# Four 128x512 reciprocals of a streaming mixer as logarithm and exponential on the activation engine

## The reference

```python
r = sigmoid(xc @ wa + ba);  i = sigmoid(xc @ wx + bx)        # xc: causal conv of the xl part, 512 wide
log_a = -8 * r * softplus(-lam);  a = exp(log_a)
mult = sqrt(-expm1(2 * log_a))
h[t] = a[t] * h[t-1] + mult[t] * i[t] * xc[t]                # linear recurrence over tokens
y_lru = h * gelu(gl)
hm = rmsnorm_per_head(mlstm_chunk(q, k, v, gates))           # 4 heads of 128
y_m = hm * mlstm_norm * sigmoid(o)
x = x + concat(y_lru, y_m) @ w_out
x = x + peer(rmsnorm(x))                                     # 8 heads, each the top 16 of 16384 experts
```

## Time and profile before

| | |
|---|---|
| time of three runs | median 3380.85 us (3374.79, 3380.85, 3388.64) |
| the profiled execution | 3388.64 us, span 3386.7 us |
| mean granted clock of TensorE in it | 0.976 |
| busy: PE, DVE, ACT, POOL | 2947.2, 2347.8, 662.4, 2015.6 us |

### The profile page before, as it was taken

One profiled execution on the slowest core, in us unless ns is written; L12 is line 12 of the kernel. 1 busy time (PEld: TensorE's weight loads), 2 busy tenths in 40 slices (PEclk: granted clock), 3 DMA queues, 4 the chain that ended last, 5 costly groups with the idle time before them and its releaser, 6 DMA issues.

```text
span 3386.7 us, 39112 instructions
## 1 busy us (share of the span) xinstructions
PE 2947.2 (87%) x10724; PEld 1546.2 (46%) x10724; DVE 2347.8 (69%) x5813; ACT 662.4 (20%) x2015; POOL 2015.6 (60%) x2132
## 2 busy tenths in 40 slices
PE   7687899888998899878998899888998899988777
PEld 2462464345543464445543455435543455444223
DVE  3474986678756886678756886578756786679553
ACT  2211221112211221112211122112211122111111
POOL 0133566656667566666667566665667566765775
PEclk9798999999999999999999999999999999999999
DMA  7455999999999999999999999999999999999998
GB/s 256 144 180 201 401 343 353 403 382 383 343 379 413 363 359 345 408 385 388 339 378 416 372 356 336 398 388 372 343 379 402 375 356 335 393 418 385 414 420 331
DMA packets 340167, 1213.76 MB, mean 358 GB/s; under 512 B 41072, under 2 KB 41200, under 8 KB 339904
## 3 DMA queue, kind: packets, MB, share of 16 engines
q0 software_dynamic: 304128, 1107.43, 85.0%
q1 hardware_dynamic: 35776, 103.32, 7.9%
HBM read 1205.73 MB, written 4.87 MB: 357 GB/s over the span
## 4 chain that ended last, share of the span: by engine, by line
PE 44%; DMA 19%; DVE 18%; issue 11%; POOL 4%; ACT 2%; POOLq 0%; DVEq 0%; SPq 0%; ACTq 0%
PE acc L428 27%; PE bank L428 17%; DMA ring<-peer_v,idx 16%; DVE ring L1272 5%; POOL ring L404 4%; DMA ring<-peer_u,idx 4%; ACT xn L755 1%; DVE kw L1056 1%; DVE xn L1167 1%; DVE xn L1170 1%; DVE topi L1058 1%; DVE eh L1067 1%; DVE kw L1066 1%; DVE tops L1057 1%; DVE bank L1180 1%
## 5 line engine op out<-in xcount | busy, mean ns | idle before, releaser
L428 PE MATMUL acc<-ring,diag 128*128 128x512 f32 (+1 forms) x4224 | 2039.6, 611 | 351.9 <-DMA ring<-peer_v,idx 225.8
L1272 DVE SCALAR_TENSOR_TENSOR ring<-ring,xcur 128x1024 f32<-128x1024 f32 x1056 | 1281.0, 1218 | 657.5 <-DMA ring<-peer_u,idx 648.6
L404 POOL DMA_INDIRECT ring<-peer_u,idx x1056 | 1016.0, 962 | 736.3 <-issue 284.8
L404 POOL DMA_INDIRECT ring<-peer_v,idx x1056 | 995.9, 943 | 614.5 <-issue 272.9
L428 PEld LDWEIGHTS acc<-ring,diag 128*128 128x128 f32 (+1 forms) x4224 | 731.8, 189 | 1312.1 <-issue 894.1
L755 ACT ACTIVATE diag<-ident,coef 128x128 f32<-128x128 f32 x1024 | 368.4, 395 | 618.3 <-PE acc L428 521.5
L428 PEld LDWEIGHTS bank<-xT,win 128*128 128x128 f32 (+1 forms) x2304 | 273.9, 184 | 76.6 <-issue 67.7
L428 PE MATMUL bank<-xT,win 128*128 128x128 f32 (+1 forms) x2304 | 284.9, 279 | 2.4 <-ACT xT L755 2.4
L755 ACT ACTIVATE G<-bank 128x128 f32<-128x128 f32 (+1 forms) x137 | 40.6, 296 | 667.0 <-PE bank L428 666.8
L428 PE MATMUL bank<-win,xT 128*128 128x512 f32 (+3 forms) x368 | 165.6, 581 | 1.9 <-ACT xT L755 1.9
L428 PEld LDWEIGHTS bank<-xT,qk 128*128 128x128 f32 x1024 | 130.1, 199 | 35.9 <-issue 35.9
(11 more groups left out here) (227 smaller groups left out, 1847.1 us busy)
## 6 DMA issues: line engine op xcount, KB each, us to landing
qk<-wq SPq DMA_DIRECT2D x64, 512.0 KB, 6.8
t<-wq SPq DMA_DIRECT2D x64, 512.0 KB, 6.6
ring<-peer_u,idx POOLq DMA_INDIRECT x1056, 6.3
ring<-peer_v,idx POOLq DMA_INDIRECT x1056, 6.3
win<-w_in SPq DMA_DIRECT2D x6, 2048.0 KB, 15.3
ring<-wq SPq DMA_DIRECT2D x16, 512.0 KB, 4.9
wout<-w_out SPq DMA_DIRECT2D x1, 4096.0 KB, 22.1
xn<-x_prompt SPq DMA_DIRECT2D x8, 512.0 KB, 9.2
```

The lines of the kernel that those rows point to most:

```text
L404: pool.indirect_dma_start(out=ring[:, slot, :], out_offset=None, in_=(peer_u, peer_v)[which], in_offset=bass.IndirectOffsetOnAxis(ap=idx[: ...
L428: return nc.tensor.matmul(out, lhsT, rhs, start=start, stop=stop)
L1272: stt(row, row, 1.0, xcur[:, :], ALU.mult, ALU.mult, accum_out=dots[:, column(b, e):column(b, e) + 1]).then_inc(s_dot, 1)
```

## The change

Each of the four reciprocals of 1 + e^-x over 128x512 (GELU, r, i, output gate) is taken from DVE. DVE still adds 1 (for three of them, with a clamp to 2^60 in the same instruction; for the GELU the 1 is the bias of the logarithm), and ACT computes exp(-ln(1 + e^-x)) in place. The chain behind r and i (t4, the series, the square root, the scan) and ACT's square root move two ticks later, ACT's exponential of the decay one tick later, the product with the GELU one tick later, and the add for the output gate five ticks earlier. The code is otherwise the same, two semaphores for each of i and the output gate are new (s_ri1, s_i, s_o1, s_so).

```diff
+            def logistic(t, bias):
+                link(a(t, t, ACT.Ln, bias=bias))
+                return a(t, t, ACT.Exp, scale=-1.0)
...
                 if full and tick == T_GELU + 2:
                     act.wait_ge(s_gl_arg, w + 1)
-                    a(t3[:, :, 0:n], t3[:, :, 0:n], ACT.Exp, scale=GELU_SCALE).then_inc(s_gl_exp, 1)
+                    link(a(t3[:, :, 0:n], t3[:, :, 0:n], ACT.Exp, scale=GELU_SCALE))
+                    logistic(t3[:, :, 0:n], 1.0).then_inc(s_gl_exp, 1)
...
                 if tick == T_LRU + 3:
-                    act.wait_ge(s_r, v + 1)
+                    act.wait_ge(s_ri1, v + 1)
+                    link(logistic(t1[:, :, 0:n], 0.0))
+                    act.sem_inc(s_r, 1)
+                    logistic(t2[:, :, 0:n], 0.0).then_inc(s_i, 1)
+                if tick == T_LRU + 4:
                     for f in range(FT):
                         last = a(t3[:, f, 0:n], t1[:, f, 0:n], ACT.Exp, scale=decay_c[:, f:f + 1])
                     last.then_inc(s_a, 1)
...
-                if tick == T_LRU + 10:
+                if tick == T_LRU + 12:
                     act.wait_ge(s_m2, v + 1)
...
+                if full and tick == T_CHUNK + 10:
+                    act.wait_ge(s_o1, w + 1)
+                    logistic(sigo[0:n, :, :], 0.0).then_inc(s_so, 1)
...
-                    ts(t3[:, :, 0:n], t3[:, :, 0:n], -50.0, None, ALU.max).then_inc(s_gl_arg, 1)
-                if full and tick == T_GELU + 3:
+                    ts(t3[:, :, 0:n], t3[:, :, 0:n], -26.0, None, ALU.max).then_inc(s_gl_arg, 1)
+                if full and tick == T_GELU + 4:
                     dve.wait_ge(s_gl_exp, w + 1)
-                    link(ts(t3[:, :, 0:n], t3[:, :, 0:n], 1.0, None, ALU.add))
-                    link(dve.reciprocal(t3[:, :, 0:n], t3[:, :, 0:n]))
                     link(tt(G[:, :, 0:n], G[:, :, 0:n], t3[:, :, 0:n], ALU.mult))
...
                 if tick == T_LRU + 2:
                     dve.wait_ge(s_ri_exp, v + 1)
-                    link(ts(t1[:, :, 0:n], t1[:, :, 0:n], 1.0, None, ALU.add))
-                    dve.reciprocal(t1[:, :, 0:n], t1[:, :, 0:n]).then_inc(s_r, 1)
-                if tick == T_LRU + 3:
-                    link(ts(t2[:, :, 0:n], t2[:, :, 0:n], 1.0, None, ALU.add))
-                    link(dve.reciprocal(t2[:, :, 0:n], t2[:, :, 0:n]))
-                if tick == T_LRU + 4:
+                    ts(t1[:, :, 0:n], t1[:, :, 0:n], 2.0 ** 60, 1.0, ALU.min, ALU.add)
+                    ts(t2[:, :, 0:n], t2[:, :, 0:n], 2.0 ** 60, 1.0, ALU.min, ALU.add).then_inc(s_ri1, 1)
+                if tick == T_LRU + 6:
                     dve.wait_ge(s_r, v + 1)
+                    dve.wait_ge(s_i, v + 1)
...
+                if full and tick == T_CHUNK + 8:
+                    dve.wait_ge(s_o, w + 1)
+                    ts(sigo[0:n, :, :], sigo[0:n, :, :], 2.0 ** 60, 1.0, ALU.min, ALU.add).then_inc(s_o1, 1)
...
                 if tick == T_CHUNK + 13:
-                    dve.wait_ge(s_o, w + 1)
-                    link(ts(sigo[0:n, :, :], sigo[0:n, :, :], 1.0, None, ALU.add))
-                    link(dve.reciprocal(sigo[0:n, :, :], sigo[0:n, :, :]))
+                    dve.wait_ge(s_so, w + 1)
```

More of the change, by code:

```diff
@@ L207, in program @@
         s_gl_ps, s_gl, s_gl_arg, s_gl_exp = sem("s_gl_ps"), sem("s_gl"), sem("s_gl_arg"), sem("s_gl_exp")
-        s_ri_ps, s_ri_exp, s_r, s_a, s_m2, s_mult, s_lru = (sem(f"s_{n}") for n in ("ri_ps", "ri_exp", "r", "a", "m2", "mult", "lru"))
+        s_ri_ps, s_ri_exp, s_ri1, s_i, s_r, s_a, s_m2, s_mult, s_lru = (sem(f"s_{n}") for n in ("ri_ps", "ri_exp", "ri1", "i", "r", "a", "m2", "mult", "lru"))
         s_q_ps, s_q, s_k_ps, s_k, s_v_ps, s_v = (sem(f"s_{n}") for n in ("q_ps", "q", "k_ps", "k", "v_ps", "v"))
@@ L212, in program @@
         s_kt_ps, s_kw, s_s_ps, s_p, s_num_ps, s_num, s_c_ps, s_c = (sem(f"s_{n}") for n in ("kt_ps", "kw", "s_ps", "p", "num_ps", "num", "c_ps", "c"))
-        s_o_ps, s_o, s_hsq, s_hrs, s_ym, s_ym_ps, s_ymT = (sem(f"s_{n}") for n in ("o_ps", "o", "hsq", "hrs", "ym", "ym_ps", "ymT"))
+        s_o_ps, s_o, s_o1, s_so, s_hsq, s_hrs, s_ym, s_ym_ps, s_ymT = (sem(f"s_{n}") for n in ("o_ps", "o", "o1", "so", "hsq", "hrs", "ym", "ym_ps", "ymT"))
         s_out_ps, s_h2, s_rstd2, s_xn2, s_x2_ps, s_x2 = (sem(f"s_{n}") for n in ("out_ps", "h2", "rstd2", "xn2", "x2_ps", "x2"))
@@ L1165, in mixer @@
                     dve.wait_ge(s_ri_exp, v + 1)
-                    link(ts(t1[:, :, 0:n], t1[:, :, 0:n], 1.0, None, ALU.add))
-                    dve.reciprocal(t1[:, :, 0:n], t1[:, :, 0:n]).then_inc(s_r, 1)
-                if tick == T_LRU + 3:
-                    link(ts(t2[:, :, 0:n], t2[:, :, 0:n], 1.0, None, ALU.add))
-                    link(dve.reciprocal(t2[:, :, 0:n], t2[:, :, 0:n]))
-                if tick == T_LRU + 4:
+                    ts(t1[:, :, 0:n], t1[:, :, 0:n], 2.0 ** 60, 1.0, ALU.min, ALU.add)
+                    ts(t2[:, :, 0:n], t2[:, :, 0:n], 2.0 ** 60, 1.0, ALU.min, ALU.add).then_inc(s_ri1, 1)
+                if tick == T_LRU + 6:
                     dve.wait_ge(s_r, v + 1)
+                    dve.wait_ge(s_i, v + 1)
                     link(tt(t4[:, :, 0:n], t1[:, :, 0:n], spread(decay_c[:, FT:2 * FT].unsqueeze(2), 2, n), ALU.mult))
                     tt(t2[:, :, 0:n], t2[:, :, 0:n], xc[:, :, 0:n], ALU.mult)
-                if tick == T_LRU + 5:
+                if tick == T_LRU + 7:
                     link(ts(by4(bA)[:, :, 0:n], t4[:, :, 0:n], 1.0 / 120, None, ALU.mult))
-                for at, c in ((5, -1.0 / 24), (6, 1.0 / 6), (6, -0.5), (7, 1.0)):
+                for at, c in ((7, -1.0 / 24), (8, 1.0 / 6), (8, -0.5), (9, 1.0)):
                     if tick == T_LRU + at:
                         link(stt(by4(bA)[:, :, 0:n], by4(bA)[:, :, 0:n], c, t4[:, :, 0:n], ALU.add, ALU.mult))
-                if tick == T_LRU + 7:
+                if tick == T_LRU + 9:
                     link(ts(t4[:, :, 0:n].bitcast(u32), t4[:, :, 0:n], 0.125, None, ALU.is_lt))
-                if tick == T_LRU + 8:
+                if tick == T_LRU + 10:
                     dve.wait_ge(s_a, v + 1)
@@ L1186, in mixer @@
                     link(ts(t1[:, :, 0:n], t1[:, :, 0:n], -1.0, 1.0, ALU.mult, ALU.add))
-                if tick == T_LRU + 9:
+                if tick == T_LRU + 11:
                     link(dve.copy_predicated(t1[:, :, 0:n], t4[:, :, 0:n].bitcast(u32), by4(bA)[:, :, 0:n]))
                     ts(t1[:, :, 0:n], t1[:, :, 0:n], 2.0 ** -60, None, ALU.max).then_inc(s_m2, 1)
-                if tick == T_LRU + 11:
+                if tick == T_LRU + 13:
                     dve.wait_ge(s_mult, v + 1)
@@ L1198, in mixer @@
                     link(last)
-                if tick == T_LRU + 12:
+                if tick == T_LRU + 14:
                     last = dve.tensor_copy(hst[:, :].unsqueeze(2), t4[:, :, n - 1:n])
```

## The result

The changed kernel takes 3391.33 us (median of 20 runs, 3380.88 to 3398.06), the kernel before 3380.26 us (20 runs): ratio 1.003, 95% interval 1.002 to 1.0041. It is a little slower, by 0.2 to 0.4%. The forecast was 3364 us with a range up to 3384; the result is outside it, on the side of the rival called slower, but not by that rival's mechanism. The profiled execution has a span of 3395.4 us, 8.7 us more than that of before.

A forecast was written before the change was run, and what follows sets the result against it. PE was taken to bound ticks 43 to 82 of a block, POOL's gather pace the last block. The terms +9.5 - 15.6 - 3 - 5.7 - 2 gave -16.8 us, 3364 us against the median 3380.85, range 3336 to 3384.

The forecast's parts named there:

- the rival called slower: New wait at tick 59 throttles TensorE's clock in every block: +2 us, up to +12.5 us (3393 us); chance 0.08.
- DVE loses: Four reciprocals and an add leave DVE per full mixer: 13.8 us in each of eight, 111 us busy time, mostly not gain.
- the likeliest range of the forecast: The main case, with the change -8 to -27 us faster; chance 0.62, half of it on either side of the 0.5% line.
- r and i, tick 59: ACT's added work delays a diagonal; PE's wait grows from 0.42 to about 1.8 us a block, +9.5 us over seven blocks.
- Tick 64: PE's wait there for DVE's late dots, about 2.2 us in each of seven blocks, goes: -15.6 us.
- Clock: Half-clock pieces after three tick-64 waits go, new tick-59 waits may bring one or two: -2 us (bounds -5 and +6).
- Output gate: POOL no longer waits for DVE at tick 87: -3 us of at most -5.4 over the loop, as PE bounds again soon after.
- Ahead of the loop: In the three mixers before the loop, reciprocals leave the serial chain, less a later diagonal: -5.7 us in sum.
- GELU and the chain behind r: ACT's longer GELU at tick 53 and the chain moved by two ticks are hidden in the loop: 0 us.
- DVE is the real bound: DVE's queue, not PE, sets the pace in ticks 43 to 82; half the possible gain is 37 us, 3338 us; chance 0.12.
- Given back: Tick-59 wait costs what tick 64 saves, POOL's gain is lost, only the start remains: 0 to -7 us, 3377 us; chance 0.18.
- The list of what would make the prediction wrong: Dot 63 not earlier, PE waiting at another diagonal (54, 68 or 85), or loop blocks shrinking by more than 3.7 us each.

The follow-up runs named there:

- e1: Changed kernel with 12 idle semaphore increments ahead of DVE's loop, restoring the loop top's old place 488; 3370.53 us, ratio 0.9961 to the kernel before.
- e8: Changed kernel with 60 idle semaphore increments ahead of DVE's loop, its top at place 536; 3368.3 us, ratio 0.995 to the kernel before.
- e11: Changed kernel with 6 idle semaphore increments ahead of DVE's loop, its top at place 482; 3366.22 us in one execution.
- e6: Kernel before with only r and i moved to ACT, plus 6 idle increments putting DVE's loop top at place 488; 3369.45 us, ratio 0.9963.
- e5: Changed kernel with r and i back on DVE, plus 6 idle increments putting DVE's loop top at place 488; 3385.59 us, ratio 0.9999.
- e4: e1 with ACT's logarithms and exponentials of r and i one tick earlier, at tick 57; 3349.36 us, ratio 0.9906 to the kernel before.
- e3: Changed kernel with 12 idle semaphore increments at the end of DVE's loop body, its top not moved; 3392.54 us in one execution.
- e12: Changed kernel with 120 idle semaphore increments ahead of DVE's loop, its top at place 596; 3382.78 us in one execution.
- e2: Kernel before, otherwise unchanged, with 116 idle semaphore increments ahead of DVE's loop, its top at place 604; 3422.42 us, ratio 1.0109.

## Why the prediction was wrong

**The step that failed** is the first of the change part by part, "DVE loses": its instructions were priced by their durations alone (111 us of busy time, "most of this is not gain"), and that there are also fewer of them had no term anywhere in the sum. 12 fewer ahead of the loop moved the target of DVE's jump to the end of a piece and cost 31 us at the six jumps. The sum without it was -16.8; with the place of the target restored (e1) or at other good places (e8, e11) the changed kernel is 11.4, 14.5 and 13.4 us below the kernel before, timed beside it (medians of e1 and e8, one execution of e11). That lies within the likeliest range of the forecast (-8 to -27), but in part by luck: by the prediction's terms r and i alone were to give 4 us and GELU and output gate 10, and they gave 13 and none (e6, e5), so that two misses of 9 and 10 us cancel. The terms, one by one:

- *r and i, tick 59*: forecast a wait of 1.8 us; 1.8 us in all seven blocks, 10.0 us more than before where 9.5 was forecast. Right. That it was a loss that need not be, e4 shows.
- *Tick 64*: forecast gone, -15.6 us; gone in all seven, 15.7 us. Right.
- *Clock*: taken as -2 us with -5 as the bound. From tick 56 to 74 the loss of granted clock (one minus the clock, summed over seven blocks) is 5.1 us before and 0.0 in the changed kernel, in e1, e6, e8 and e11; e5, which has the old wait at tick 64, has 5.1. The bound was the value: none of the new waits brought a half-clock piece. Block 4, ticks 56 to 74, before and after (the third column from the right is the granted clock):

```profile
2024.00:2079.00 55.00, 52.25 (x208) 30.57 (x207) 41.23 (x69) 11.71 (x36) 33.37 (x35) 0.97 0.92 338
```

```profile
2029.00:2083.00 54.00, 52.16 (x243) 32.80 (x242) 36.73 (x71) 18.19 (x49) 34.52 (x36) 1.00 0.97 352
```

By the Trainium skill (TensorE: Matmul & The Clock Gate, HAM oscillation), weighed in the prediction, a wait in every iteration can bring the low clock in every iteration; the trace does not agree for these waits of 1.8 us; it agrees for the longer ones at the jump (last section). Ticks 53 to 72 are 17.0 us shorter over seven blocks in the changed kernel and 14.7 to 17.1 in e1, e8, e11 and e6, where waits and clock together give 10.0 - 15.7 - 5.1 = -10.8. What gives the other 4 to 6 us was not separated. It is the greater part of what the prediction lacked for r and i.
- *Output gate*: forecast -3 us of a possible 5.4. POOL's wait at tick 87 goes as forecast, and is given back by tick 104 (e5, above): 0. Ticks 82 to 104 together take 1.0 us more over the seven blocks in the changed kernel, 5.2, 6.2 and 2.6 more in e1, e5 and e8, and 2.0 less in e11. The guess that half of it stays was the error.
- *Ahead of the loop*: forecast -5.7 us. PE's waits for the normalised heads are 4.0 and 3.8 us shorter, 3.7 was forecast. The first dot of block 0 comes 4.2 us earlier, and 7.7, 1.7, 6.4, 1.4 and 6.2 in e1, e3, e8, e11 and e12, which have the same program up to there: -4.6 in the mean. Right, within a scatter as large as the term. In e5, where -7.5 was forecast, it was -1.4 in its one trace.
- *GELU and the chain behind r*: forecast 0. Ticks 43 to 53 and 72 to 82 are within 1.4 and 0.3 us over seven blocks. Right.

Of the rivals, "DVE is the real bound" is out: with 110 us of DVE's work gone and the top at a good place the gain is 11 to 15 us, not 37. "Given back" (0 to -7 us) is missed by less, and POOL's gain is given back as it had it. "Slower" came true in its sign alone; its mechanism, a throttled clock behind tick 59, did not occur. The list of what would make the prediction wrong had the diagonals of ticks 54, 68 and 85, and not that of tick 16. The trace of before had the sign of it, unread: the row of L1289 above, with 31.4 us of idle time, 9.2 of them under "issue", and the row of ACT's exponential:

```profile
L755 ACT ACTIVATE gl_a<-gl_a 128x16 f32<-128x16 f32 x66 | 14.1, 214 | 308.0 <-DVE gl_a L1281 279.0 <-issue 28.9
```

They say that at the jump the engines wait for something that is no other engine's work, some 4.8 us each time (28.9 / 6). That the size of the code ahead of the loop has a price could be asked from there, but only the runs show it.

The Trainium skill has the rule that I passed over (Runtime: NRT & Kernel Launch, Instruction fetch mechanics): a taken branch whose target is not in the window of fetched pages makes the engine wait for a fetch of the target's page. The traces agree, with 3.4 to 5 us until the first work behind the jump and 4.75 us more until the next piece (e12). The page gives blocks of 16 KiB, 256 instructions; the packets that are more where DVE stands are of 8192 bytes, and the padding repeats at 128 (476 and 604 slow), so here the measurement decides.

## What to carry to other kernels

Where a long loop body is jumped back to, an edit ahead of it moves the loop's top within the fetched pieces, and that alone moved this kernel by 21 to 28 us (e1; e2 without its increments), more than the 11 to 15 us that the edit was worth. So look for "issue" at the first instruction of the body in every trace, count how many instructions an edit adds or removes ahead of the loop, and before a small difference is put down to the edit, time it with a handful of idle instructions as padding; a kernel left slow by its edit may be a gain in disguise. And where a wait for an in-order engine is bought with an edit, try to move the work by one tick first: here that was worth 21 us (e4 against e1), more than the edit.

## What the runs showed of the hardware

- DVE's instructions come in pieces of 128 (476 and 604 slow, 536 not), and packets of 8192 bytes carry them. After a jump back, the first work came 3.4 to 4.8 us after the last (3.35 in e1, 4.75 in e12, ACT 4.50 and 4.96), with a DMA share of 0.71 and 0.79 (last rows below); the next piece came 4.75 us behind the first (e12, block 3; 3.8 to 5.0 over its six jumps). DVE stood for it as soon as the first was used up; the work done in the meantime is all that hides it.
- The cost is a step, not a slope, over most of a piece: places 479, 482, 488 and 536 are alike, 596 costs some 15 us over six jumps (2.5 us each by the dots), 476 and 604 some 30.
- Increments of a semaphore are not free: 116 of them on DVE stretched the one gap they stood in from 7.1 to 19.4 us, some 0.1 us each.
- PE's wait at the jump is followed by half-clock work in both kernels. The first sum behind it takes 3.4 to 3.8 us at all six jumps (3.78 in the row of block 3 above), where a sum at full clock takes 1.98; PE had waited 4.1 to 5.6 us before it in the kernel before and 8.1 to 11.0 in the changed one. The granted clock of the 10 us behind the wait costs 14.9 us in the six blocks before and 13.4 after, so the clock is no part of the loss. The windows of block 3, both of which end ahead of that sum, have 1.00 before and 0.75 after (third column from the right; the DMA share is the second), but most of the second window is the wait itself, in which PE has nothing to do:

```profile
1507.00:1518.00 11.00, 4.17 (x10) 1.37 (x9) 5.57 (x21) 2.74 (x6) 7.00 (x8) 1.00 0.71 219
```

```profile
1512.00:1530.00 18.00, 5.66 (x8) 1.79 (x8) 5.38 (x21) 2.74 (x6) 7.50 (x8) 0.75 0.79 277
```
